# Dot products of the prompt tiles that read their token operand from PSUM instead of SBUF, in a two-layer decoder step on one core

## The reference, cut to what matters

```python
q = (xb @ wq).astype(jnp.float32).reshape(PEER_BLOCK, PEER_HEADS, 2, PEER_HALF)
s = jnp.einsum('thcd,chkd->thck', q, keys)
sv, si = lax.top_k(s, PEER_TOPK)
...
top, sel = lax.top_k(cand, PEER_TOPK)
eidx = jnp.take_along_axis(cidx, sel, axis=-1)
gate = jax.nn.softmax(top, axis=-1)
ue = u_tab[eidx]
act = jax.nn.gelu(jnp.einsum('td,thkd->thk', xb, ue).astype(jnp.float32))
ve = v_tab[eidx]
return jnp.einsum('thk,thkd->td', (gate * act).astype(xb.dtype), ve)
```

## Time and profile before

| | |
|---|---|
| median of 3 runs | 1908.96 us (1907.51 to 1915.76) |
| the profiled execution | 1909.85 us, of which the span is 1908.0 us |
| busy over the span | PE 989.2, DVE 1017.8, POOL 1126.3, ACT 173.8 us |
| moved by DMA | 687.23 MB, mean 360 GB/s |
| u phases, by the first and last dot of the tile (trace) | tile 0: 119 to 380; tile 1: 602 to 825; tile 3: 1065 to 1277; tile 4: 1510 to 1687 |

### The profile page before, as it was taken

How to read it: one execution, slowest core, us unless ns; L and a number is a source line. 1 busy time by engine, 2 the same in 40 slices (tenths; PEclk the granted TensorE clock), 3 DMA queues, 4 the chain that set the end, 5 groups by cost and what they waited for, 6 DMA issues and landing times.

```text
span 1908.0 us, 17956 instructions
## 1 busy us (share of the span) xinstructions
PE 989.2 (52%) x6274; PEld 461.0 (24%) x6274; DVE 1017.8 (53%) x2806; ACT 173.8 (9%) x297; POOL 1126.3 (59%) x1062
## 2 busy tenths in 40 slices
PE   7867411059866462068655776017894520045546
PEld 4434201024422221043111343004341110021113
DVE  1257899932562759755500486883265379960001
ACT  2222110000100110001000022000010000000001
POOL 0033465763567657853577776774456677767770
PEclk9898755579978685588778977557996765567888
DMA  7586787999999999998999999999998999999993
GB/s 295 182 306 265 294 300 290 371 352 415 387 397 401 412 415 344 324 367 313 374 405 409 407 405 408 314 391 361 404 388 331 391 411 409 410 409 409 409 409 123
DMA packets 173191, 687.23 MB, mean 360 GB/s; under 512 B 19856, under 2 KB 21520, under 8 KB 158366
## 3 DMA queue, kind: packets, MB, share of 16 engines
q0 software_dynamic: 152064, 553.72, 75.2%
q1 hardware_dynamic: 21038, 132.37, 17.8%
HBM read 679.88 MB, written 6.59 MB: 360 GB/s over the span
## 4 chain that ended last, share of the span: by engine, by line
DMA 28%; POOL 26%; PE 20%; DVE 13%; issue 11%; ACT 1%; SPq 0%; POOLq 0%; DVEq 0%; ACTq 0%
POOL rows L1196 26%; PE bank L740 9%; DMA rows<-in_v,index_tb 8%; PE acc L1022 7%; DMA rows<-in_v,index_ta 5%; DMA rows<-in_u,index_A 5%; DMA rows<-in_u,index_B 5%; DVE rows L1796 4%; DMA wring<-in_w 3%; DVE scratch L1584 1%; PE bank L737 1%; DMA rows<-in_u,index_S 1%; PE bank L942 1%; DVE scratch L1736 1%; PE bank L987 1%
## 5 line engine op out<-in xcount | busy, mean ns | idle before, releaser
L1196 POOL DMA_INDIRECT rows<-in_u,index_A x256 | 310.4, 1213 | 275.2 <-DVE index_A L1771 183.7
L1022 PE MATMUL acc<-rows,wz 128*32 128x512 f32 x2048 | 325.6, 768 | 205.4 <-DMA rows<-in_v,index_tb 137.5
L740 PE MATMUL bank<-wring,turned 128*128 128x512 f32 x832 | 400.2, 631 | 37.4 <-DMA wring<-in_w 30.8
L1196 POOL DMA_INDIRECT rows<-in_v,index_ta x256 | 245.6, 960 | 199.3 <-PE acc L1022 133.2
L1196 POOL DMA_INDIRECT rows<-in_u,index_B x256 | 294.6, 1151 | 108.8 <-issue 71.6
L1796 DVE SCALAR_TENSOR_TENSOR rows<-rows,xn_b 128x1024 f32<-128x1024 f32 x256 | 308.6, 1225 | 68.5 <-DMA rows<-in_u,index_B 62.6
L1796 DVE SCALAR_TENSOR_TENSOR rows<-rows,xn_a 128x1024 f32<-128x1024 f32 x256 | 306.8, 1225 | 69.1 <-DMA rows<-in_u,index_A 64.5
L1196 POOL DMA_INDIRECT rows<-in_v,index_tb x256 | 240.8, 941 | 142.3 <-issue 66.0
L740 PEld LDWEIGHTS bank<-wring,turned 128*128 128x128 f32 x832 | 161.5, 202 | 235.1 <-issue 198.6
L1022 PEld LDWEIGHTS acc<-rows,wz 128*32 128x32 f32 x2048 | 70.5, 128 | 420.0 <-issue 415.8
L987 PE MATMUL bank<-xn_s,consts 128*128 128x128 f32 x256 | 33.8, 297 | 228.6 <-DVE rows L1791 145.4
(11 more groups left out here) (293 smaller groups left out, 1021.2 us busy)
## 6 DMA issues: line engine op xcount, KB each, us to landing
wring<-in_w SPq DMA_DIRECT2D x108, 1024.0 KB, 8.3
scratch<-in_c_s SPq DMA_DIRECT2D x2, 2064.0 KB, 11.7
out_c_s<-scratch SPq DMA_DIRECT2D x2, 2064.0 KB, 12.8
rows<-in_u,index_A POOLq DMA_INDIRECT x256, 7.9
rows<-in_v,index_ta POOLq DMA_INDIRECT x256, 7.7
rows<-in_u,index_B POOLq DMA_INDIRECT x256, 13.0
rows<-in_v,index_tb POOLq DMA_INDIRECT x256, 7.8
keys<-in_keys SPq DMA_DIRECT2D x2, 1024.0 KB, 9.4
```

Of the source, the lines that this page charges most:

```text
L740: ins = pe.matmul(ps[:, :], turned["A"][:, 4 * h + c, :], w[:, c, :], start=first, stop=end, skip_group_check=True)
L1022: ins = pe.matmul(acc[i * QUAD:(i + 1) * QUAD, c, :], wz[:, i, g * QUAD:(g + 1) * QUAD], row, start=first, stop=end, skip_group_check=True)
L1196: pool.indirect_dma_start(out=rows[:, n % RING, :], out_offset=None, in_=a[table], in_offset=bass.IndirectOffsetOnAxis(ap=which[:, at:at + ...
```

## The change

A new group, "show", stands ahead of the dots of each prompt tile (tiles 0, 1, 3, 4). In it ScalarE copies the tile's normed tokens, 128 x 1024 float32, from `xn` into `acc`, once the tokens are written and the sum of the tile before has been read out of `acc`. The dots of that tile wait for it once, and read `acc` in place of `xn`. Nothing else of the computation differs. The planner is told of the group (1.2 us on ACT, what it needs, when it may be placed).

```diff
@@ groups_of
     for t in PASS_TILES[p]:
+        if KIND[t] != "S":
+            out.append(("show", t))
         out += [("dots", t, g) for g in range(ROWS_U[KIND[t]] // DOTS)]
@@ ready_for
+    if kind == "show":
+        return ("norm", t, "turn2") in placed
@@ STEPS, NEEDS
+"show": (("ACT", 1.2),)
-"dots": ("norm",)
+"dots": ("norm", "show"), "show": ("norm",)
@@ Clocks.first
+        if stage == "show" and t:
+            ready = max(ready, self.done["add", t - 1])
@@ woven
-        elif groups[0][0] in ("gelu", "weights", "add"):
+        elif groups[0][0] in ("show", "gelu", "weights", "add"):
             take = "group" if of_group[1] <= of_stage[1] + 0.5 else "stage"
@@ scalar
+            def show(t):
+
+                act.wait_ge(xn_scaled, count(("show",), ("show", t)))
+                if t > 0:
+                    act.wait_ge(acc_read, t)
+                after(act.activation(acc[:, :, :], xn[KIND[t]][:, :].rearrange("p (c n) -> p c n", c=2), ACT.Copy), xn_shown)
@@ vector, norm
-                        step(scaled)
+                        after(scaled, xn_scaled)
@@ vector, take_dots
                 kind = KIND[t]
+                if kind != "S" and g == 0:
+                    dve.wait_ge(xn_shown, count(("show",), ("show", t)))
@@ vector, take_dots
-                        u = rows[:, n % RING, :]
-                        dve.scalar_tensor_tensor(u, u, 1.0, xn[kind][:, :], ALU.mult, ALU.mult,
+                        u = rows[:, n % RING, :].rearrange("p (c n) -> p c n", c=2)
+                        dve.scalar_tensor_tensor(u, u, 1.0, acc[:, :, :], ALU.mult, ALU.mult,
                                                  accum_out=dots[kind][:, s:s + 1]).then_inc(u_used, 1)
```

More of the change, by code:

```diff
@@ L250 @@
     "turn3": (("PE", 1.4), ("ACT", 1.2)), "gate": (("PE", 3.4), ("ACT", 0.8)), "embed": (("PE", 4.5), ("DVE", 3.4)),
-    "final": (("ACT", 1.7),), "add": (("DVE", 1.3),), "dots": (("DVE", 1.31 * DOTS),), "vals": (("PE", 1.8),)}
+    "final": (("ACT", 1.7),), "add": (("DVE", 1.3),), "show": (("ACT", 1.2),), "dots": (("DVE", 1.31 * DOTS),), "vals": (("PE", 1.8),)}
 SMALL = {
@@ L272 @@
     "query": ("turn2", "norm"), "turn_pq": ("query",), "match": ("turn_pq",), "rank": ("match",), "sources": ("rank",), "pairs": ("rank", "sources"),
-    "best": ("pairs",), "soften": ("best",), "choose": ("soften",), "turn_index": ("choose",), "turn_s": ("choose",), "dots": ("norm",),
+    "best": ("pairs",), "soften": ("best",), "choose": ("soften",), "turn_index": ("choose",), "turn_s": ("choose",), "dots": ("norm", "show"), "show": ("norm",),
     "gelu": ("dots",), "weights": ("gelu",), "vals": ("weights", "gelu"), "add": ("vals",), "turn3": ("add",), "gate": ("turn3",), "embed": ("gate",),
@@ L644, in build @@
         wz_clear, xn_ready, squared = sem("wz_clear"), sem("xn_ready"), sem("squared")
+        xn_scaled, xn_shown = sem("xn_scaled"), sem("xn_shown")
         vector_step, scalar_step = sem("vector_step"), sem("scalar_step")
@@ L1386, in _ @@
                   "match": match_keys, "soften": soften, "turn3": turn3, "gate": gate,
-                  "final": final, "gelu": gelu}
+                  "final": final, "show": show, "gelu": gelu}
             for e in SCHEDULE:
```

## The result

The changed kernel takes 1860.23 us (median of 4 runs, 1858.91 to 1863.42) against 1912.08 for the kernel before (4 runs, 1907.51 to 1915.76): ratio 0.974, 95% interval 0.9711 to 0.9768 (the quotient of the two medians is 0.973), some 50 us less. The forecast was 1876, its range 1858 to 1900, so the time lies 2 us inside its lower end. The profiled execution took 1858.91 us, its span is 1857.1. Lines have moved by a few: the gather is L1203, the dot L1812, the add L1845, the copy L1367.

A forecast was written before the change was run, and what follows sets the result against it. Gathers held while DVE dots with two SBUF operands run were taken to slow the u phases. 1909.85 - 36 us for the four tiles + 3.5 for the copies = 1877.4, 0.9 above the median, so 1876; range 1858 to 1900.

The forecast's parts named there:

- the third rival: In the u phases, the stretch comes from the dot's write to `rows` or its length; only costs remain, 1913 us; chance 0.05.
- The gathers: u-phase gathers drop to 0.94 us, POOL's period to 1.24, so DMA (1.28) or DVE (1.145 a dot) sets the pace.
- Tile 1: u phase from 740 us: 59.5 dots in 85 us would take 68 at 1.145; bound 17 us, 15 taken.
- Tile 3: u phase from 1204 us: 52.5 dots in 73 us would take 60; bound 10 us after other DVE work, 9 taken.
- Tile 0: u phase, DVE nearly full with ranking, gains only what DVE idles; bounds 8 and 14 us, 10 taken.
- Tile 4: u phase, 410 GB/s nearly throughout; only 1510 to 1520 is short, a gain of 2 us.
- The copy and the wait: Four ACT copies of 1.1 us ahead of the dots, first dots about 1.25 us later; cost 0 to 9 us, 3.5 taken.
- The dot: A u-phase dot reading PSUM was taken to last as long as the SBUF one, by the add's 1221 ns; cost 0.
- The first rival: Dearer PSUM dots in the catch-up stretches: every 1.21 us loses 12 us, 1888; 1.28 loses 25, 1901; chance 0.10.
- the fourth: Rival: DVE restarts at the second bank, a u-phase dot takes 1.46 us, total 1953; decides from about 1.37; chance 0.04.
- the second rival: Tiles 1 and 3 end 24 us sooner, but TensorE, a weight load or the planner's list loses half the gain: 1894; chance 0.12.
- The order: The new entry shifts the planner's clocks by at most 1.2 us a pass; effect 0, with 5 us either way.

## Why the prediction was right, step by step

**The bound and its cause.** Right, and shown by taking the operand alone back (0.9999). So the third rival, that the change does not do what it says, is out. By what the Trainium skill, "SBUF — State Buffer", section "Who interferes with whom", infers for tensor_tensor, which takes the read interface where the writing of descriptors needs the write interface, nothing would have been won; the traces disagree, 1.99 us beside a dot of two SBUF inputs against 0.94 beside one with PSUM, in the same kernel otherwise, and 1.26 beside a tensor_tensor (below). The rule of the same section that two SBUF inputs contend with a GpSimd instruction that reads SBUF fits the traces; that a gather's reading of its indices is what is held is not shown.

**The gathers** are 939 and 938 ns, forecast 940 to 1000. Of 1056 gathers 8 are over 1.1 us, each beside another DVE instruction with two SBUF inputs, as here in the timeline after (before there were 173):

```profile
710.23 0.69 DVE L1644 TENSOR_TENSOR mixer<-mixer,h_inv 128x512 f32<-128x512 f32 x1
710.47 1.26 POOL L1203 DMA_INDIRECT rows<-in_u,index_B  x1 [0.30 <-DVE rows L1812]
```

**The sum was too small**, 36 - 3.5 = 33 against about 50 (50.9 between the two traces): the bound was right, the size was off by a third. Of the 18 us that are missing 11 lie in tiles 1 and 3 (tiles 0 and 4, 2 more and 2 less, cancel out), 3.5 are the copies, and 3.5 lie outside the phases (first dot 2.4 us earlier, tail 1.9 shorter), no more than two executions of one kernel differ by. That 1860 is in the range has some luck in it: its lower end, 1858, stood for all bounds taken in full and no cost at all, and the bounds of tiles 1 and 3 were themselves too low.
- Tile 1: 15 forecast, 21.7 measured, above the 17 that I called the bound from DVE. The stretch was the right one: up to 740 the kernel before ran at full rate. The step that failed is that I held fixed how many dots lie in it. With gathers that keep step, DVE gets ahead earlier: 138 us into the phase 74 dots have begun, where it was 70, so 4 x 1.145 = 4.6 us of dots have left the stretch, and 17 + 4.6 = 21.6. On top I had taken off 2.
- Tile 3: 9 forecast with 10 as bound, 13.6 measured. Here 139 us into the phase nearly as many dots have begun as before (77, where it was 76), and 73 - 60 = 13 was the bound before I took off 2 to 3 us for other DVE work and 1 more. That work was there in the kernel before (2.8 us in 1204:1278), but not in the same place after: in the window after DVE spends 59.28 of 60 us on dots, 0.5 on anything else. The 1 more was asked for by no row.
- Tile 0: 10 forecast, 12.1 measured, inside 8 to 14.
- Tile 4: 2 forecast, 0 measured in the one trace. Its first 10 us (1461:1471) now run at 411 GB/s instead of 331, and yet the phase is as long as before. One trace can't tell 2 us: in the six traces on the first chips whose dots of tile 4 read PSUM the phase is 170.6 to 175.9, 173 in the mean, and in the four whose dots read SBUF 174.7 to 175.8, 175 in the mean. So the 2 us may well be there.

The windows of the kernel before ahead of its two stretches, all engines:

```profile
602.00:740.00 138.00, 74.68 (x203) 39.06 (x204) 97.21 (x176) 20.77 (x31) 89.31 (x73) 0.74 1.02 409
1065.00:1204.00 139.00, 89.04 (x745) 50.07 (x743) 107.04 (x197) 28.76 (x50) 103.02 (x80) 0.79 1.02 406
```

and the windows of the dots alone after, answering to the earlier trace rows:

```profile
740.00:790.00 50.00, 49.15 (x86) 0.50 1.03 410
```

```profile
1170.00:1230.00 60.00, 59.28 (x104) 0.50 1.03 408
```

Priced by bytes at 410 GB/s instead, the stretches of the earlier trace rows give 60 x (1 - 294/410) + 26 x (1 - 377/410) = 19 us for tile 1 and 46 x (1 - 291/410) = 13 for tile 3, without a guess at where the dots come to lie: nearer to what was measured than the 15 and 9 of the sum. It does not hold everywhere: for tile 0 the same pricing gives 43 x (1 - 273/410) + 59 x (1 - 362/410) = 21 against 12.1 measured, where DVE is busy for 93 of the 102 us, and the sum's 10 by DVE's idle time was the better one. And with the right count of dots DVE's rate gives tile 1 as well (21.6).

**The copy and the wait**: 3.5 forecast, 0 measured, within what the runs can tell. The wait itself came as described (1.24 us at tile 1, copy 1.03), but the ring catches up within a few rows, and 9.5 us more of the same waits cost nothing. The upper end, 9, is not in what this kernel shows; what it left out, with 0 to 1 for tile 0, is that a copy placed behind stages that wait for TensorE costs 7 to 10 us, which the changed list avoids.

**The dot**: taken at no extra cost from the add's 1221; it is 1218, and the dots follow at 1.145. The first rival is out (it began at 1.21), and the fourth too (it wanted 1.37 or more). By the Trainium skill, "VectorE: DVE Perf Modes", section on the TRN2 errata, a dot would have been about 65 ns dearer; the trace disagrees.

**Given back**, the second rival: the stretches between the phases keep their length within 1.4 us and the tail gains 1.9, so nothing is on the chips that move 409 GB/s. On chip 6 something of its kind is seen in tile 3's phase, where TensorE is late instead. **The order**: forecast 0 with 5 either way; 0 measured, by the old order with the early copy against the changed kernel on one chip.

## What to carry to other kernels

Look at how long an instruction of a DMA-issuing engine takes beside each kind of VectorE instruction: one with two SBUF inputs held a gather of 0.94 us to 1.99, and a copy of one operand into two idle PSUM banks, 1.03 us of a free engine, ended it. Price a stretch that it slows both by its bytes, against the rate of a stretch with nothing in the way, and by the next engine's pace: here bytes came near for tiles 1 and 3 (19 and 13 against 21.7 and 13.6) and far too high for tile 0, where other work shares DVE (21 against 12.1). Don't hold fixed how much of its work lies in the stretch. And where a copy is added that others wait for, look at what stands ahead of it in its engine's queue: the same copy, 27 us later, cost 7 to 10 of some 50 us.

## What was not expected of the hardware

- One kernel took 2021 us on one chip and 1908 to 1912 on the others, 6% apart, with 367 GB/s in a v phase that the others run at 409; whether the chip or something beside it does this is open. A change worth 2.6% on the one kind was worth at most 0.5% on the other (one kernel, ratio 0.9977), although three of its four phases gained there too: the fourth lost some 20 us while TensorE stood at small matmuls.
- A copy of 128x1024 from SBUF to PSUM on ACT takes 1028 ns, a little less than the square of that size from SBUF to SBUF (1057).
- A VectorE instruction of 128x1024 whose operand crosses two PSUM banks starts every 1.145 us, just as with SBUF.
